# Eight query-projection units in one round of a sparse attention, and its second compressed half a round earlier

## The reference, cut to what matters

```python
qg = h @ w_qg
q = (qg[..., :N_HEADS * dh] * (dh ** -0.5)).reshape(bsz, seq, G, HPG, dh)
gates = jax.nn.sigmoid(qg[..., N_HEADS * dh:]).reshape(bsz, seq, G, HPG, 3)
# per head: compressed, selected, window
s = jnp.einsum("bqghd,bngd->bghqn", qblk, k_cmp)
p_cmp = jax.nn.softmax(jnp.where(vis, s - slopes * (t - center), NEG_INF)) * vis
o_cmp = jnp.einsum("bghqn,bngd->bqghd", p_cmp, v_cmp)
s = jnp.where(dist >= 0, q @ k - slopes * dist, NEG_INF)
o_slc = softmax(s) @ v_slc
o_win = softmax(s_win) @ v_win
o = gblk[..., 0:1] * o_cmp + gblk[..., 1:2] * o_slc + gblk[..., 2:3] * o_win
h = h + o @ w_o
```

## Time and profile before

| | |
|---|---|
| median of 3 runs | 971.0 us (970.72 to 971.22) |
| the profiled execution: time, span | 971.74 us, 970.0 us |
| TensorE busy | 954.0 us, 98% |
| VectorE busy | 712.9 us, 73% |
| ScalarE busy | 488.6 us, 50% |
| mean granted TensorE clock | 0.996 of full |

### The profile page before, as it was taken

One profiled execution on the slowest core, in us unless ns is written; L12 is line 12 of the kernel. 1 busy time (PEld: TensorE's weight loads), 2 busy tenths in 40 slices (PEclk: granted clock), 3 DMA queues, 4 the chain that ended last, 5 costly groups with the idle time before them and its releaser, 6 DMA issues.

```text
span 970.0 us, 19340 instructions
## 1 busy us (share of the span) xinstructions
PE 954.0 (98%) x7854; PEld 919.1 (95%) x7854; DVE 712.9 (73%) x1131; ACT 488.6 (50%) x712; POOL 88.0 (9%) x132
## 2 busy tenths in 40 slices
PE   8999999999999999899999999999999999999998
PEld 8999999999999977589999999999999999999998
DVE  5886877777769878968777777698876676565654
ACT  5444644433447557847444433537667555334441
POOL 7000000000000042420000000020000000000000
PEclk9999999999999999999999999999999999999999
DMA  9846848686845762038486868435354357564611
GB/s 265 270 174 217 287 157 301 229 285 199 285 165 161 238 217 89 1 133 298 150 299 229 293 204 286 145 113 181 101 173 150 108 179 258 175 218 134 232 66 44
DMA packets 131533, 186.99 MB, mean 193 GB/s; under 512 B 6289, under 2 KB 102929, under 8 KB 131473
## 3 DMA queue, kind: packets, MB, share of 16 engines
q1 hardware_dynamic: 123984, 159.69, 49.7%
q0 software_dynamic: 6912, 25.17, 7.4%
q10 hardware_dynamic: 576, 1.29, 0.4%
HBM read 185.09 MB, written 1.05 MB: 192 GB/s over the span
## 4 chain that ended last, share of the span: by engine, by line
PE 86%; DVE 8%; ACT 3%; issue 2%; DMA 1%; POOL 1%; DVEq 0%; SPq 0%; ACTq 0%; POOLq 0%
PE ps L1898 43%; PE ps L1976 19%; PE ps L1894 12%; PE ps L1896 4%; DVE g_lo L1174 1%; ACT g_hi L668 1%; DMA g_raw<-in_w_up 1%; PE ps L1946 1%; PE ps L2095 1%; PE ps L2042 1%; DVE rstd L1230 1%; PE ps L2160 1%; DVE ybuf L1194 1%; PE ps L2175 1%; DVE e_even L1541 1%
## 5 line engine op out<-in xcount | busy, mean ns | idle before, releaser
L1898 PE MATMUL ps<-opa_hi,g_hi 128*128 128x256 f32 x864 | 230.1, 287 | 1.3 <-ACT opa_hi L717 1.1
L1898 PE MATMUL ps<-opa_lo,g_hi 128*128 128x256 f32 x864 | 220.8, 283 | 0.0
L1898 PE MATMUL ps<-opa_hi,g_lo 128*128 128x256 f32 x864 | 182.8, 284 | 0.0
L1292 DVE TENSOR_TENSOR g_lo<-g_raw,g_hi 128x2048 fp32r<-128x2048 f32 x54 | 123.8, 2293 | 69.0 <-ACT g_hi L742 69.0
L1898 PEld LDWEIGHTS ps<-opa_hi,g_hi 128*128 128x128 f32 x864 | 166.5, 193 | 4.6 <-issue 4.1
L1898 PEld LDWEIGHTS ps<-opa_lo,g_hi 128*128 128x128 f32 x864 | 162.4, 192 | 0.1
L1976 PE MATMUL ps<-hid_hi,d_hi 128*128 128x256 f32 x528 | 147.8, 280 | 1.8 <-DVE hid_lo L1295 1.7
L1976 PE MATMUL ps<-hid_hi,d_lo 128*128 128x256 f32 x528 | 147.5, 279 | 0.0
L1976 PE MATMUL ps<-hid_lo,d_hi 128*128 128x256 f32 x528 | 147.4, 279 | 0.0
L1174 DVE TENSOR_TENSOR g_lo<-g_raw,g_hi 128x2048 fp32r<-128x2048 f32 x54 | 123.6, 2289 | 30.9 <-ACT g_hi L668 30.5
L1898 PEld LDWEIGHTS ps<-opa_hi,g_lo 128*128 128x128 f32 x864 | 139.8, 193 | 0.0
(11 more groups left out here) (340 smaller groups left out, 1809.4 us busy)
## 6 DMA issues: line engine op xcount, KB each, us to landing
g_raw<-in_f_w_gu SPq DMA_DIRECT2D x44, 1024.0 KB, 8.7
ada_raw<-in_w_ada POOLq DMA_DIRECT2D x48, 512.0 KB, 6.3
d_raw<-in_f_w_down SPq DMA_DIRECT2D x22, 1024.0 KB, 5.1
g_raw<-in_w_in SPq DMA_DIRECT2D x14, 1024.0 KB, 8.3
g_raw<-in_w_gate SPq DMA_DIRECT2D x11, 1024.0 KB, 7.2
g_raw<-in_w_up SPq DMA_DIRECT2D x11, 1024.0 KB, 9.7
d_raw<-in_w_down SPq DMA_DIRECT2D x11, 1024.0 KB, 5.3
g_raw<-in_a_w_in SPq DMA_DIRECT2D x10, 1024.0 KB, 8.3
```

The source lines that it names most:

```text
L1292: dve.tensor_tensor(part_view(g_lo, g0 + r, True), raw_cols(c % 2, r % 2, True), part_view(g_hi, g0 + r, True).bitcast(F32), ALU.subtract) ...
L1898: mm = pe.matmul(pair(b)[:, a, :], wt[:, a * P:(a + 1) * P], xt, **st)
```

## The change

On TensorE all eight units of the fourth query step are issued in the third round, two at a time (units 8 and 9, 10 and 11, 12 and 13, 14 and 15), where four were; the fourth round keeps none of its four. `compressed_scores(1)`, with the wait for `evac_q(3)` ahead of it, moves from the fifth round to the fourth, between the two turns. `compressed_turn(1)` moves from the seventh round to the sixth, and the sixth round's extra order (turn ahead of values) goes. The wait for `evac_q(2)` ahead of `scores(4)` goes too; `query_units` has the same wait at unit 8. VectorE's `evac_q(3)`, `compressed_shift(1)` and `compressed_factors(1)` and ScalarE's `compressed_exp(1)` and `compressed_copy(1)` each move one `j` earlier. The instructions are the same in number and shape.

```diff
@@ -897,7 +897,7 @@
                 act.activation(pct[:, q, :], ps[:, 6 if q else 7, 0:T], ACT.Copy).then_inc(pct_made, 1)
 
             for j in range(1, NH // 2 + 2):
-                if j == 5:
+                if j == 4:
                     compressed_exp(1)
                 if 1 < j < NH // 2:
                     exps(j, 0)
@@ -1582,18 +1582,18 @@
                 for e in range(2):
                     if j < NH // 2 + 1:
                         normalize(2 * j - 2 + e)
-                    if j == 4 and e == 0:
+                    if j == 3 and e == 0:
                         evac_q(3)
                     if j < NH // 2:
                         shift(2 * j + e)
-                if j == 5:
+                if j == 4:
                     compressed_factors(1)
                 dve.wait_ge(opa_hi_made, 8 * A_FILL["attn"] + j - 1)
                 dve.tensor_tensor(opa_lo[:, j - 2, :], ps[:, 7, 0:T],
                                   opa_hi[:, j - 2, :].bitcast(F32), ALU.subtract).then_inc(opa_made, 1)
                 if j == 3:
                     split_g(WO)
-                if j == 4:
+                if j == 3:
                     compressed_shift(1)
                 if j == 8:
                     split_g(WO + 1)
@@ -2197,44 +2197,36 @@
 
             scores(2)
             compressed_turn(0)
-            query_units(8, 1)
+            query_units(8, 2)
             values(0)
-            query_units(9, 1)
+            query_units(10, 2)
             turn(1, 0)
-            query_units(10, 1)
+            query_units(12, 2)
             turn(1, 1)
-            query_units(11, 1)
+            query_units(14, 2)
 
             scores(3)
-            query_units(12, 2)
             values(1)
-            query_units(14, 1)
             turn(2, 0)
-            query_units(15, 1)
+            pe.wait_ge(g_evac, evacs(QG + 3))
+            compressed_scores(1)
             turn(2, 1)
 
-            pe.wait_ge(g_evac, evacs(QG + 2))
             scores(4)
             values(2)
             turn(3, 0)
-            pe.wait_ge(g_evac, evacs(QG + 3))
-            compressed_scores(1)
             turn(3, 1)
 
             scores(5)
+            compressed_turn(1)
             values(3)
             turn(4, 0)
             turn(4, 1)
 
             for j in (5, 6):
                 scores(j + 1)
-                if j == 5:
-                    compressed_turn(1)
-                    turn(j, 0)
-                    values(j - 1)
-                else:
-                    values(j - 1)
-                    turn(j, 0)
+                values(j - 1)
+                turn(j, 0)
                 turn(j, 1)
 
             out_units(0, 0, 2)
```

## The result

The changed kernel takes 973.09 us (median of 18 runs, 971.88 to 974.47), the kernel before 971.05 us (18 runs, 968.90 to 972.61). The ratio is 1.0020 with a 95% interval of 1.0013 to 1.0026, so the change costs 2.0 us, between 1.3 and 2.5. The profiled execution took 974.15 us, 2.4 us more than that of before.

A forecast was written before the change was run, and what follows sets the result against it. VectorE sets the pace from scores(3) on; its stretch shrinks from 33.62 to 32.08 us but starts 2.84 later, ending 1.3 later. With 0.81 for the clock: 971.0 + 2.1 = 973.1 us, range 971.4 to 974.5.

The forecast's parts named there:

- The four units lie on the path, 2.84 us: Third round: it has no gap, so four added units delay scores(3) by 2.84 us and shift(6) starts at 382.39.
- evac_q(3) is hidden and leaves 0.72 us behind: VectorE: moved one turn earlier, evac_q(3) falls in the wait for scores(3), a gain of 0.72 us.
- VectorE's stretch of 32.08 us, and 0.81 for the clock: VectorE, shift(6) to the eighth round's low part: 33.62 us becomes 32.08, plus 0.81 if scores(5) runs at low clock.
- The fifth round's idle time, and a fall of the clock: TensorE idles about three of five microseconds between values(2) and scores(5); clock expected to fall again, priced at 0.81 us.
- rival 2: VectorE's later start alone, +1.3 us, 972.3; low clock lies in TensorE's idle time or costs as before; chance 0.32.
- From the profiled execution to the median: Whole kernel: profiled 971.74 us against median 971.0; whether or not timed executions hold the low stretch, the change adds 2.1.
- my first road: Timed executions also hold the low stretch; the change adds 1.3 + 0.81 = 2.1 us if scores(5) is slowed too.
- The second road: Timed executions mostly lack the low stretch, so 1.3 was counted against a kernel they beat by 0.81; difference again 2.1.
- TensorE as the pace setter (4): Fourth to eighth rounds: TensorE, not VectorE, ends the rounds, so the change is faster, 969.1 us; chance 0.08.
- Clock low twice in a row (3): Fifth round's idle time: a second 3.4 us at 1.2 GHz could cover scores(6), another 0.8 to 0.9; about 974; chance 0.15.
- The lower end of my range, 971.4: Whole kernel's time: range said to start a little under half-way between 969.1 and 972.3, at 971.4 us.
- rounds seven and eight would be as before: Attention's last two rounds: a sign to look for in the trace, claiming they stay unchanged.

The follow-up runs named there:

- the two kernels with three units less: Units 12 to 14 left out of the kernel before (fourth round), ratio 0.9995, and out of the changed kernel (third round), ratio 1.0003.
- The units alone: Kernel before with all eight units in the third round, compressed half and evac_q(3) left in place; 974.14 us, ratio 1.0038.
- the filler: Changed kernel plus 18 matmuls with unread results in TensorE's idle time of the fifth round; 973.25 us, ratio 1.0022.
- the early split: Changed kernel with the split of the first output step's weights moved ahead of scores(3), ScalarE's part one turn sooner; ratio 1.0009.
- the compressed half alone: Changed kernel with units back to four and four, the second four right behind scores(3); compressed half stays one round sooner; 973.21 us, ratio 1.0019.

## Why the prediction was right, step by step

The forecast was 973.1 us and the median is 973.09. The mechanism was right: a later start of VectorE's stretch, which is not made up, and a low clock at scores(5). That the number fits to a hundredth is luck: the difference itself is known only to 1.3 to 2.5 us, and in the traces two terms of the sum missed in opposite directions, the work by 0.2 us too little and the clock by 0.2 to 0.5 us too much.

*The four units lie on the path, 2.84 us.* shift(6) was to start at 382.39; it started at 382.36. That little of it is paid back is borne out by the two kernels with three units less. One reading on the way was wrong: I wrote that VectorE waits in the third and in the fourth round, but in the third it is busy for 7.91 of 8.09 us, and its wait of 1.39 us lies in the fourth. The term does not rest on it.

*evac_q(3) is hidden and leaves 0.72 us behind.* It starts at 380.78 and is done 0.9 us before scores(3) releases shift(6). The units alone, where it is not hidden, have the longer attention span, 46.12 us, and cost 0.7 to 1.0 us more at the medians than the whole change, each over the kernel before in its own series. All five of its runs have a mean clock of 0.996, and there the changed kernel's median is 973.44 us, 0.7 less than 974.14. Five runs are few.

*VectorE's stretch of 32.08 us, and 0.81 for the clock.* It is 415.41 - 382.36 = 33.05 us, against 32.89. The waits in it are 0.63 (clock), 0.29 and 0.15, against 0.81 and twice 0.17. So 0.2 us of the work and 0.1 of the wait for scores(6) were missed, the clock was put in 0.2 too high, and the first output unit comes at 415.68, just outside the 414.6 to 415.5 that I gave.

*The fifth round's idle time, and a fall of the clock.* Three gaps, 3.39 us in all, and one fall, from 395.5 to 398.9. Its cost to VectorE was 0.63 us in one trace and 0.35 in the other, less than the 0.81 I took. In the second the fall began at 396.0. In both it slowed scores(5), to 2.76 and 2.93 us, so the first form of my rival 2, in which the fall lies in TensorE's idle time and costs nothing, did not happen in a trace.

The Trainium skill's rule that transposes do not count as busy like products ("TensorE: Matmul & The Clock Gate", Part 4) goes with this: the fall follows transposes and idle time, and with the products of the filler there was none at this place. But they also fill the idle time, so no run here separates the two; and with the early split transposes and gaps of 0.62 and 1.85 us came before no fall at all.

*From the profiled execution to the median.* This step was the weakest. I had two cases for the kernel before, with a low stretch or without, while the runs show three levels and a few below. Each result gives the mean granted clock of the run, and each low stretch of 3.4 us takes about 0.002 off it. The runs of the kernel before in the three series of experiments, and all of the changed kernel's:

| mean clock of the run | before: runs, median us | changed: runs, median us |
|---|---|---|
| 1.000 | 22, 969.57 | none of 30 |
| 0.998 | 37, 971.00 | 8, 972.42 |
| 0.996 | 32, 972.20 | 22, 973.44 |
| 0.995 | 2, 973.65 | none |

At an equal mean clock the change costs 1.4 and 1.2 us. But a mean clock does not say where a low stretch lies, and they are not of one price. From the first output unit to the end of the span it takes 556.4 to 556.8 us in the eight traces with a low stretch near 640 us and 555.0 in the five without, so that one costs 1.5 us, while VectorE waited 0.35 to 0.81 us for a single one in the attention. In the row of 0.998 the two kernels need not hold the same one. In the row of 0.996 both profiled executions hold both. There my first road, 1.3 + 0.81 = 2.1 us, should hold, and the runs say 1.2: that road is not borne out.

The second road compares with a kernel before that has no low stretch. My sum had taken its 0.81 us out, so against such runs the work should cost 2.1. The filled kernel is the nearest thing to the changed one at full clock: its three runs at 1.000 have a median of 971.70 us, 2.1 over the 969.57, and by the traces it is 45.21 - 42.80 = 2.4. The low stretches cost both kernels about the same on average: 971.17 - 969.57 = 1.6 us (the mean of 93 runs against the first row) and 973.19 - 971.70 = 1.5 us (1.3 against the mean of the three). So the second was the better: work at full clock costs 2.1 us, and the clock nets out. That rests on three runs of the filled kernel and is not shown as firmly as the rest. Why the difference is only 1.2 us where both kernels are at 0.996 stays open; the low stretches would have to cost the kernel before 0.9 us more there than the changed one, and no trace shows that.

*The rivals.* TensorE as the pace setter (4) is out by the filler and by the early split. Rival 2 had a second form, a low stretch as costly before as after, and that is what the averages show; but 1.3 us is the new kernel without a low stretch against the old one with its 0.81. With the same cost in both, my own terms give 2.1, so the 972.3 did not belong to this form, and the price of the rival was wrong there. Clock low twice in a row (3) happened in the traces of the compressed half alone and of the changed kernel with three units less, for 6.8 us each, but not in the traces of the changed kernel. The lower end of my range, 971.4, does not lie half-way between 969.1 and 972.3 as I wrote, which is 970.7. I was wrong to say that rounds seven and eight would be as before. The seventh is 6.08 us instead of 7.00, since the compressed factors no longer delay it. The sum is not touched: they stay in VectorE's stretch.

## What to carry to other kernels

An engine that is busy for 98% of the span need not be the one whose queue sets the pace of a stage: here 2.1 us of filler work on it, in the right place, did not make the stage longer. Before moving independent work between rounds, ask for each round which engine ends it, and put the work where the bound engine's partner waits; the kernel that gained, 1 to 2 us by the medians and 0.4 to 0.7 at an equal mean clock, moved 2.3 us of the pacing engine's own work into its wait and left the matmuls alone. And where runs of one kernel differ by some tenths of a per cent, sort them by the granted clock of each run before comparing, and find in the traces what a low stretch costs at each place.

## What the runs showed of the hardware that I had not expected

Executions of the same kernel have no, one or two low stretches of the clock, 3.4 us at 1.2 GHz each. Of the 13 traces two have none, and the kernel before has its medians at 969.57, 971.00 and 972.20 us, 1.2 to 1.4 us apart, for the mean clocks 1.000, 0.998 and 0.996. A stretch can follow directly on another (394.5 to 401.3 us with the compressed half alone); VectorE then waited 1.57 us for scores(5), where a single one cost it 0.81 at most, and 1.00 us for scores(6), where it waits 0.29 us with the clock at its upper level. And the low stretch near 640 us comes and goes with no edit near it: the changed kernel has it in one of its two traces and not in the other, and the time from the first output unit to the end of the span is 556.7 us with it and 555.0 without.
